# State-space decay rows and attention scores as pairs of 64-row matmuls, a further look-ahead of one pair of heads, and a down projection that waits per gated tile

## What is computed

```python
for i in range(DEPTH_2):                       # 0: griffin_swa, 1: mamba2
    h = h + rms_norm(mixer(rms_norm(h, pre), *mix), post)
    h = h + rms_norm(conv_ffn(rms_norm(h, f_pre), w_up, c_w, c_b, w_down), f_post)

# layer 0, windowed attention: 16 query heads of 64, 2 key heads, window 128, meta tokens, sinks
s_band = jnp.einsum("bnqkgd,bnskd->bnkgqs", qb, k_band) * scale
# layer 1, state space: 32 heads of 64, 8 groups, blocks of 128 tokens
seg = cs_t[..., :, None] - cs_t[..., None, :]
decay_in = jnp.exp(jnp.where(tril, seg, -jnp.inf))
y_diag = jnp.einsum("bcgls,bcghls,bcsghp->bclghp", cb, decay_in, xdt)
# feed-forward
return (jax.nn.gelu(g, approximate=True) * up) @ w_down      # 2816 = 22 tiles of 128
```

## Time and profile before

| | |
|---|---|
| median of three executions | 2697.47 us (2692.95 to 2702.48) |
| the profiled execution | 2703.03 us, span 2701.2 us |
| mean granted clock of TensorE | 0.954 |
| busy: TensorE, VectorE, ScalarE, GpSimd | 2430.9, 762.1, 555.8, 49.5 us |
| windowed attention | about 1724 to 1792 us |
| decay loop | about 2308 to 2372 us |
| starts of the down projections | 2029 and 2611 us |

### The profile page before, as it was taken

How to read it: one execution, slowest core, us unless ns; L and a number is a source line. 1 busy time by engine, 2 the same in 40 slices (tenths; PEclk the granted TensorE clock), 3 DMA queues, 4 the chain that set the end, 5 groups by cost and what they waited for, 6 DMA issues and landing times.

```text
span 2701.2 us, 36383 instructions
## 1 busy us (share of the span) xinstructions
PE 2430.9 (90%) x15128; PEld 1614.7 (60%) x15128; DVE 762.1 (28%) x1853; ACT 555.8 (21%) x1381; POOL 49.5 (2%) x71
## 2 busy tenths in 40 slices
PE   6999997898997978979887778999999999999998
PEld 4685875586442423334323226777887788678887
DVE  1010345532121111111111014733440335624431
ACT  2110112411121211112111113532111221512110
POOL 0000000000000000000000000100000000100000
PEclk9999998997998999999989878989999999989999
DMA  8132252053999998999999994323334333023432
GB/s 319 62 125 94 89 193 107 29 200 142 391 411 421 410 421 371 392 421 420 421 420 421 421 411 178 110 78 124 141 116 145 129 142 139 32 78 126 155 114 90
DMA packets 86935, 608.36 MB, mean 225 GB/s; under 512 B 9552, under 2 KB 11728, under 8 KB 16080
## 3 DMA queue, kind: packets, MB, share of 16 engines
q1 hardware_dynamic: 86224, 602.49, 56.4%
q0 software_dynamic: 400, 2.46, 0.2%
q10 hardware_dynamic: 144, 1.05, 0.1%
HBM read 604.91 MB, written 1.05 MB: 224 GB/s over the span
## 4 chain that ended last, share of the span: by engine, by line
PE 71%; DMA 11%; SPq 10%; DVE 4%; ACT 2%; issue 2%; DVEq 0%; POOL 0%; ACTq 0%
PE bank L532 28%; PE bank L562 10%; SPq L821 10%; PE bank L2309 8%; DMA arena<-in_w_e 7%; PE bank L546 4%; PE bank L2330 3%; DMA ring<-in_w_e 3%; PE bank L2095 2%; PE bank L2259 2%; PE bank L2484 1%; PE bank L2121 1%; DMA ring<-in_w_ada 1%; PE bank L2275 1%; PE bank L2535 1%
## 5 line engine op out<-in xcount | busy, mean ns | idle before, releaser
L532 PE MATMUL bank<-arena,ring 128*128 128x272 f32 (+3 forms) x3200 | 764.0, 401 | 6.1 <-issue 3.0
L532 PEld LDWEIGHTS bank<-arena,ring 128*128 128x128 f32 x3200 | 610.0, 191 | 153.1 <-issue 51.3
L2309 PE MATMUL bank<-arena 128*32 128x512 f32 x2184 | 276.3, 621 | 51.7 <-DMA arena<-in_w_e 51.7
L562 PE MATMUL bank<-arena,ring 128*128 128x272 f32 (+2 forms) x1216 | 280.0, 394 | 6.0 <-DVE arena L1736 6.0
L562 PEld LDWEIGHTS bank<-arena,ring 128*128 128x128 f32 x1216 | 235.9, 194 | 50.3 <-DVE arena L1736 6.9
L1605 DVE TENSOR_TENSOR arena<-bank,arena 128x256 f32<-128x256 f32 x56 | 23.7, 424 | 814.8 <-PE bank L2288 774.3
L2309 PE MATMUL bank<-ring,arena 128*32 128x512 f32 x1400 | 180.2, 626 | 39.3 <-DMA ring<-in_w_e 39.1
L2309 PEld LDWEIGHTS bank<-arena 128*32 128x32 f32 x2184 | 59.9, 111 | 205.9 <-DMA arena<-in_w_e 104.1
L1722 DVE SCALAR_TENSOR_TENSOR arena<-arena,par 128x272 f32<-128x272 f32 (+1 forms) x296 | 148.8, 503 | 10.5
L2330 PE MATMUL bank<-arena 128*32 128x256 f32 x1824 | 116.8, 401 | 27.3 <-DMA arena<-in_w_e 24.1
L1041 ACT ACTIVATE arena<-bank 32x256 f32<-32x256 f32 x224 | 83.9, 374 | 251.0 <-PE bank L2330 248.6
(11 more groups left out here) (403 smaller groups left out, 2174.5 us busy)
## 6 DMA issues: line engine op xcount, KB each, us to landing
arena<-in_w_e SPq DMA_DIRECT2D x222, 1024.0 KB, 25.4
ring<-in_w_e SPq DMA_DIRECT2D x162, 1024.0 KB, 26.0
ring<-in_w_up SPq DMA_DIRECT2D x44, 1024.0 KB, 4.8
ring<-in_w_l SPq DMA_DIRECT2D x37, 1024.0 KB, 4.8
ring<-in_w_ada SPq DMA_DIRECT2D x24, 1024.0 KB, 6.3
ring<-in_w_proj SPq DMA_DIRECT2D x24, 1024.0 KB, 4.8
ring<-in_w_down SPq DMA_DIRECT2D x32, 704.0 KB, 4.0
ring<-in_w_merge SPq DMA_DIRECT2D x16, 1024.0 KB, 4.8
```

Of the source, the lines that this page charges most:

```text
L532: mm = pe.matmul(o[:, a:n], ring[:, s, k * 256 + c * P:k * 256 + (c + 1) * P], rhs(k), start=(k == 0), stop=(k == KT - 1))
L562: mm = pe.matmul(o[:, a:n], ring[:, s, k * P:(k + 1) * P], rhs(part * kt + k), start=(part == 0 and k == 0), stop=(part == parts - 1 and k ...
L2309: mm = pe.matmul(bank[q * GROUP:(q + 1) * GROUP, hidden_bank(g), :], xe[:, (g // CHUNK) % 2, k, s:s + GROUP], w[:, q * 512:(q + 1) * 512], ...
```

## The change

Four edits. (1) The down projections wait for gated tile k ahead of matmul k of the first output, instead of for all tiles at the start. (2) The keys are kept once, `k0`, both key heads on their own 64 partitions; the scores of the two heads of a pair are matmuls over 64 partitions each, issued alternately, and stand ahead of the values of pair j-2. The clears are gone. (3) The decay rows of two heads are matmuls over 64 partitions each, from `csr` and a copy of it on partitions 64 to 95, into four banks; rows 2n+4 and 2n+5 are issued in step n, and both wait for the decays of heads 2n and 2n+1. (4) One matmul and one ScalarE copy more make the copy of `csr`.

```diff
-ROW_BANKS = (2, 3, 6)
+ROW_BANKS = (2, 3, 6, 7)
...
-            for s in range(2):
-                ins = act.activation(kz[64 * s:64 * s + 64, s, :], o[64 * s:64 * s + 64, 0:L], ACT.Copy)
-            ins.then_inc(free, 1)
+            act.activation(k0[:, :], o[:, 0:L], ACT.Copy).then_inc(free, 1)
...
             act.wait_ge(sem("dt_step"), 6)
+            act.activation(csr[64:64 + SH, :], bank[64:64 + SH, 4, 0:L], ACT.Copy)
...
-            pool.memset(kz[64:128, 0, :], 0.0).then_inc(sem("kz_cleared"), 1)
-            pool.memset(kz[0:64, 1, :], 0.0).then_inc(sem("kz_cleared"), 1)
-            pool.wait_ge(sem("kz_cleared"), 2)
...
-                pe.wait_ge(sem("ffn_act"), at.ffn)
                 at.a = a2
-                project_deep(pe, at, 2, FT // 2, lambda k: actF[:, k, a2:], L, done=result_sum, a=a2)
+                project_deep(pe, at, 2, FT // 2, lambda k: actF[:, k, a2:], L, done=result_sum, a=a2,
+                             first=lambda k: pe.wait_ge(sem("ffn_act"), at.ffn - FT + k + 1))
...
+            def swa_scores(j):
+                if j >= 1:
+                    pe.wait_ge(sem("swa_masked"), 2 * j)
+                if j < 8:
                     pe.wait_ge(sem(f"bank_read{(q_read + j) % NL}"), (q_read + j) // NL + 1)
+                for t0 in (0, P) if j < 8 else (0,):
+                    for s in range(2):
+                        half = slice(64 * s, 64 * s + 64)
+                        if j < 8:
+                            mm = pe.matmul(bank[:, (2 * j + s) % 3, t0:t0 + t0 + P], q0[half, j, t0:t0 + P], k0[half, 0:t0 + P],
+                                           start=True, stop=True)
...
                 if j >= 1:
                     swa_turn(2 * j - 2)
+                if j < 9:
+                    swa_scores(j)
                 if j >= 2:
                     swa_values(j - 2)
-                if j < 9:
-                    swa_scores(2 * j)
                 if j >= 1:
                     swa_turn(2 * j - 1)
-                if j < 9:
-                    swa_scores(2 * j + 1)
...
             pe.wait_ge(sem("dt_step"), 4)
+            pe.matmul(bank[64:64 + SH, 4, 0:L], ident[0:SH, 0:SH], csr[0:SH, :], start=True, stop=True)
...
-            def ssm_rows(h):
+            def ssm_ready(h):
...
-                if h >= 3:
-                    pe.wait_ge(sem("ssm_decay"), h - 2)
+                if h >= 4:
+                    pe.wait_ge(sem("ssm_decay"), h - 3)
+
+            def ssm_row_pair(heads):
+                for h in heads:
+                    ssm_ready(h)
                 for c, (t0, n) in enumerate(TOK[0:2]):
+                    for h in heads:
+                        half = slice(64 * (h % 2), 64 * (h % 2) + 64)
+                        mm = pe.matmul(bank[:, ROW_BANKS[h % 4], SEG[c]:SEG[c] + L - t0],
+                                       cst("ident", 64 * (h % 2) + h, 1)[half, :].to_broadcast([64, P]), csr[half, t0:L],
+                                       start=True, stop=True)
+                        if c == 1:
+                            mm.then_inc(sem("ssm_rows"), 1)
...
-            for h in range(3):
-                ssm_rows(h)
+            ssm_row_pair((0, 1))
+            ssm_row_pair((2, 3))
             for n in range(ST):
-                for h in (2 * n + 3, 2 * n + 4):
-                    if h < SH:
-                        ssm_rows(h)
+                if n < ST - 2:
+                    ssm_row_pair((2 * n + 4, 2 * n + 5))
                 pe.wait_ge(sem("ssm_weights"), 2 * n + 2)
```

More of the change, by code:

```diff
@@ L733, in program @@
         q0 = take(KT, T)
-        kz = take(2, L)
+        k0 = take(L)
         q_end = take(8, META)
@@ L1312, in _ @@
                 act.activation(d[:, 144:288], d[:, 144:288], ACT.Exp, bias=csc[:, 0, h:h + 1])
-                act.activation(d[:, 288:416], bank[:, ROW_BANKS[h % 3], 288:416], ACT.Exp, bias=csc[:, 0, h:h + 1])\
+                act.activation(d[:, 288:416], bank[:, ROW_BANKS[h % 4], 288:416], ACT.Exp, bias=csc[:, 0, h:h + 1])\
                    .then_inc(sem("ssm_decay"), 1)
@@ L1897, in ssm_clamp @@
                 dve.tensor_tensor(dec[:, h % DECAYS, 0:288].rearrange("p (a b) -> p a b", a=2),
-                                  bank[:, ROW_BANKS[h % 3], 0:288].rearrange("p (a b) -> p a b", a=2),
+                                  bank[:, ROW_BANKS[h % 4], 0:288].rearrange("p (a b) -> p a b", a=2),
                                   csp[:, :, h:h + 1].to_broadcast([P, 2, 144]), ALU.min).then_inc(sem("ssm_clamped"), 1)
@@ L2539, in _ @@
             q_read = at.out
[L2541 to L2546, removed]
-                    pe.wait_ge(sem(f"bank_read{(q_read + j) % NL}"), (q_read + j) // NL + 1)
[L2548 to L2552, removed]
+            def swa_scores(j):
+                if j >= 1:
+                    pe.wait_ge(sem("swa_masked"), 2 * j)
+                if j < 8:
+                    pe.wait_ge(sem(f"bank_read{(q_read + j) % NL}"), (q_read + j) // NL + 1)
+                for t0 in (0, P) if j < 8 else (0,):
[4 more added lines that the diff above has]
+                                           start=True, stop=True)
+                        else:
+                            mm = pe.matmul(bank[:, (2 * j + s) % 3, 0:L], q_end[half, :, :].rearrange("p j t -> p (j t)"),
+                                           k0[half, :], start=True, stop=True)
+                        if t0 == P or j == 8:
+                            mm.then_inc(sem("swa_scores"), 1)
             def swa_turn(i):
@@ L2577, in swa_values @@
                 mm.then_inc(sem("swa_pv"), 1)
-            pe.wait_ge(sem("kz_cleared"), 2)
             for j in range(10):
@@ L2650, in ssm_rows @@
                     pe.wait_ge(sem("cb_read"), 1)
-                if h >= 3:
-                    pe.wait_ge(sem("ssm_decay"), h - 2)
-                for c, (t0, n) in enumerate(TOK[0:2]):
-                    mm = pe.matmul(bank[:, ROW_BANKS[h % 3], SEG[c]:SEG[c] + L - t0],
-                                   cst("ident", h, 1).to_broadcast([P, P]), csr[:, t0:L],
-                                   start=True, stop=True)
-                mm.then_inc(sem("ssm_rows"), 1)
+                if h >= 4:
[3 more added lines that the diff above has]
+                    ssm_ready(h)
+                for c, (t0, n) in enumerate(TOK[0:2]):
+                    for h in heads:
[5 more added lines that the diff above has]
+                            mm.then_inc(sem("ssm_rows"), 1)
             def group_sum(n):
```

## The result

The changed kernel takes 2672.11 us (median of four executions, 2669.44 to 2673.34); the kernel before, timed on the same chip, took 2697.81 (2692.95 to 2702.48). The ratio is 0.9904, with a 95% interval of 0.9884 to 0.9923. In microseconds, one minus the ratio times 2697.8, that is 25.9 us less, with an interval of 20.8 to 31.3. The forecast was 21.1 us less, 2676.4.

What follows compares the result with a forecast made beforehand. TensorE, busy 90% of the span, was taken as the bound, with a circle of waits in the decay loop. Savings 7.7 + 9.8 - 0.6 + 4.2 = 21.1 us off 2697.5 gave 2676.4 us, range 2667 to 2690.

Steps and rivals of the forecast that it cites:

- The circle of 3.61 us: Decay loop before: values and group sum, row, clamp, weights, values wait on each other in turn, 3.61 us.
- Part 1: Down projections: per-tile waits remove 6.0 us of standstill and 1.7 us of half clock, 7.7 us saved.
- Part 2: Pairs of 64 rows: two heads cost what one does, 0.8 us in the loop; each tile-shape change costs 0.1.
- the rival price of about 0.4 us: Tile-mode change drains one whole matmul, 0.4 us; each loop step loses about 0.6 more, half the gain goes.
- Part 3: Decay loop: pairs and rows issued a step earlier cut 52.0 us to 42.6; with the start, 9.8 us saved.
- the handing over: Decay loop: an allowance of 0.1 us a step for passing work between engines, making the step 3.0 us.
- VectorE's 2.6 a step: Decay loop: VectorE's 38.86 us of work in 15 steps, the next limit; as pace in every step, bound 13 saved.
- Part 4: Copy of csr for the upper rows: one more 272-column matmul where TensorE has no rest, 0.6 us lost.
- Part 5: Windowed attention: paired scores ahead of values, keys copied once; steps 6.35 instead of 6.64 us, 4.2 us saved in all.
- (a): Decay loop held by reading out and handing over, not TensorE; step 3.25 us, time 2680; chance 0.19.
- (b): The 64-row pairs don't overlap; only 2 us gained in the loop, time 2689; chance 0.06.
- (c): Granted clock falls to the lower level within the decay loop, adding 37.5 us; time 2714; chance 0.04.

Runs made afterwards that it cites:

- e5: The kernel before with the decay loop's four banks and further look-ahead, but each row still over all 128 partitions: 2691.60 us, ratio 0.9972.
- e1: The kernel before with only the down projections' wait changed to one per gated tile: 2689.04 us, ratio 0.9970.
- e3: The kernel before with only the attention part: keys kept once, paired scores ahead of the values: 2694.31 us, ratio 0.9992.
- e2: The kernel before with only the decay-loop part: 64-row pairs, four banks, one pair further ahead, copy of csr: 2680.67 us, ratio 0.9949.
- e4: The changed kernel run again without edits, on the same chip as its three separate parts: 2672.43 us, ratio 0.9905 to the kernel before.
- e10: The changed kernel run again without edits, beside the values-ahead-of-scores version: 2672.52 us, ratio 0.9912 to the kernel before.
- e8: The kernel before with only the attention order changed, both full-row scores ahead of the values: 2699.33 us, ratio 1.0009.
- e7: The changed kernel with values ahead of the paired scores again, except the last scores: 2668.93 us, ratio 0.9887 to the kernel before.
- e9: The kernel of e7 run again without edits, beside the changed kernel: 2667.18 us, ratio 0.9882 to the kernel before.
- values first: The changed kernel with attention values ahead of the paired scores except the last, run as e7 and e9: 2668.93 and 2667.18 us.
- e6: The kernel of e2 with row pairs 2n+2 and 2n+3 issued in step n, so pairing without look-ahead: 2740.12 us, ratio 1.0153 to the kernel before.

## Why the prediction was right

The range, 2667 to 2690, held the time, and the forecast was 4.3 us above it. Point by point:

**What bounds the kernel.** Right: TensorE set the pace in the loop and in attention, and each part's gain appears in the time. The circle of 3.61 us was right in size (step of 3.60 before), but it held only every second step; e5 shows that TensorE's own work, 3.89, held the others.

**Part 1, 7.7 us: measured 8.0** by the trace (3.3 + 4.7), 8.1 by e1's ratio. The whole wait went, the 44 added waits cost nothing that can be seen, and the half clock behind the second projection went with the standstill. The first projection gave 0.3 more than the 3.0 of its wait. That it shows no fall of the clock held for the kernel before; e3's fell there as well, for 3.4 us.

**Part 2, the pair at 0.8 and a change of 0.1: measured 0.91** from the pair's start to the values. Two heads cost what one does, with 0.97 us for eight records. As for the drain that the Trainium skill names (TensorEngine Tiling (Array Packing), section Tiling Modes), the run decides: it is inside that 0.91. The same columns of one head take 0.70, which leaves 0.2 at most for the change, so the rival price of about 0.4 us isn't borne out.

**Part 3, 9.8 us: measured 11.2.** The first term to be off is the four steps without a group sum: I let VectorE hold them at 2.8, 11.2 us; they took 1.98 + 3.06 + 2.28 + 3.06 = 10.38. The second is the handing over, 0.1 a step. With a pair's lead there is none, and nine steps took 26.0 us instead of 27.0. The last two, 2.67 and 1.93, were 0.25 longer than I said. Together 0.8 + 1.0 - 0.25 = 1.6 us more, and the start gave 0.2 instead of 0.4: there TensorE has a new wait of 1.0 us for VectorE's mask (line 1904) ahead of the next group's scores, the wait that I had taken to cost nothing. VectorE's 2.6 a step did not become the bound: its 37.13 us fit into 41.00. It still waited for rows, 6.3 us in all, but TensorE waited for its weights only three times.

**Part 4, 0.6 lost: measured 0.** The timeline of TensorE in the changed kernel, where the copy for the upper rows (line 2610) stands beside the 512-column matmul (line 2611):

```profile
2168.66 0.41 PE L2610 MATMUL bank<-arena,con 32*32 32x272 f32 x1
2168.67 0.60 PE L2611 MATMUL bank<-small,con 32*16 32x512 f32 x1
2168.92 0.39 PE L2610 MATMUL bank<-arena,con 32*32 32x272 f32 x1
2169.11 0.59 PE L2611 MATMUL bank<-small,con 32*16 32x512 f32 x1
...
2170.05 0.50 PE L532 MATMUL bank<-arena,ring 128*128 128x272 f32 x1
```

The first records of the two start 0.01 us apart, and the copy's second has ended (2169.31) before the other's second does (2169.70). They write to different output partitions (64 to 95, and 0 to 15), and the stretch from the first of them to the next projection is 1.39 us, as before (1.38 from the 2181.01 of the earlier trace rows). I had priced the copy as standing in line. The Trainium skill, TensorEngine Tiling (Array Packing), section Tiling Modes, says that tiles operate independently; the rows agree for two tiles that share their input rows.

**Part 5, 4.2 us: measured about 3.0.** The stage from the key copy to the first out-projection matmul takes 72.1 us before (72.5 in e1, 71.8 in e2) and 69.8, 69.9, 68.7 and 68.1 in the four kernels that have the change (the changed kernel, e4, e10, e3), 3.0 less in the mean; e3's ratio says 2.2. The term that was mis-sized is the step: 0.12 instead of 0.29. I had the scores start 0.05 us behind the end of the query copy; they start 0.14 behind it (1741.44 against 1741.12 + 0.18). And I forgot the change of shape between values and second transposes, which take 0.38, not 0.33. 5 x 0.17 = 0.85 of the 1.2 us missing. The tail, from the transposes right behind the last query tile to the out projection, is 1.6 us shorter in the mean (15.1 to 16.9 us in these four, 17.4 to 18.1 in the three before), where my terms for it make 1.85, and varies with the half clock in it. It came out about as worked: TensorE waited 2.61 us instead of 2.90, the paired last scores follow the transposes, and the second mask comes 1.14 behind the first, where it was 1.55. The changed kernel's tail in the timeline (2550 the last scores, 1803 the masks):

```profile
1772.31 0.90 PE L2562 MATMUL bank<-con,arena 128*128 128x128 f32 x3 [2.61 <-DVE arena L1821]
...
1773.14 1.28 PE L2550 MATMUL bank<-arena 64*128 64x272 f32 x4
...
1774.45 0.50 DVE L1803 SCALAR_TENSOR_TENSOR arena<-con,bank 128x272 f32<-128x272 f32 x1 [0.90 <-PE bank L2550]
...
1775.59 0.49 DVE L1803 SCALAR_TENSOR_TENSOR arena<-con,bank 128x272 f32<-128x272 f32 x1
```

**The sum.** 8.0 + 11.2 + 0 + 3.0 = 22.2 us stand in the traces, beside 25.9 by the ratio; the ratio's interval, 20.8 to 31.3, holds both. One thing that lies in between is visible. Behind the loop TensorE stands still for the reciprocal of the group norm, 2.96 us, before and after alike, and then the granted clock is 0.50. How long differs. Busy time by stretch there, first of the kernel before:

```profile
2375.00:2392.10 17.10, 16.38 (x36) 11.65 (x37) 7.58 (x17) 0.00 (x0) 0.00 (x0) 0.52 0.00 1
```

then of the changed kernel:

```profile
2352.40:2366.00 13.60, 13.60 (x31) 9.34 (x31) 6.91 (x16) 0.00 (x0) 0.00 (x0) 0.50 0.00 0
```

and of e1, which has the loop of before:

```profile
2368.60:2375.40 6.80, 6.80 (x17) 4.90 (x16) 4.66 (x12) 0.00 (x0) 0.00 (x0) 0.50 0.00 0
```

It was 17.1 us in the profiled executions of before, e3 and e8, 13.7 in the changed kernel and e7, 10.2 in e5, and 6.8 in e1, e2, e4, e9 and e10. The changed kernel and e4 are the same code and have 13.7 and 6.8, so it is not a property of the code alone. Half of it is lost time: (17.1 - 13.7) / 2 = 1.7 us of the profiled difference, up to 5.1 for the others. It may be that the change makes the short ones likelier; one profiled execution for each kernel can't show that. The mean granted clock, which is on record for all but a few of the executions, bears on it: 0.9543 over 41 of the kernel before, 0.9563 over 13 of the changed one, 0.9581 over 8 of values first. One minus the clock, times the span, is the time withheld: 123, 117 and 112 us, give or take 1 to 2. The stretch behind the second down projection makes 1.7 us of the first difference of 6. So the changed kernel seems to run at a slightly higher clock elsewhere too. By an estimate from all these executions, among those of one kernel 1 us more withheld goes with some 0.3 us more time; the other 4 to 5 us would then make some 1.4 of the 3.7 us between the traces and the ratio. In which stretches they lie, and what makes up the rest, stays open.

**The rivals.** (a) did not happen: no value matmul waits for weights except three times, once early and at the last two pairs, 1.6 us in all. (b) did not happen; e5, which comes close to it, gains 4.1 us in the loop where I had said 2 for (b). (c) did not happen to this kernel. It did to e6, where TensorE works at half clock through most of the loop; the loop of 80 us that my price meant (42.6 + 37.5) became 99.8 there, since at the lower clock the circle grows too, which (c) had left out.

## What to carry to other kernels

When matmuls use only half of the input rows, two of them on different halves and into different banks cost what one costs (0.97 us for either here); but take the lead first, because a pair is one lump of work, and a loop that pairs without issuing a step further ahead may stand still longer than it saves. Put a matmul whose operand another engine has just begun to copy behind work that is ready, not ahead of it: values before scores made each attention step 0.38 us shorter than the reverse. Where an accumulation takes its tiles in the order in which they are made, a wait for all of them can become a wait for each tile in the first output, and what it saves is the wait and the half clock behind it (3.0 + 1.7 us at the second projection).

## What the runs showed of the hardware

- A loop in which TensorE stood still 2 to 3 us in each step of 5 to 8 us ran at a mean granted clock of 0.59 and took 99.8 us for work that takes 41.0 with 1.6 us of standstill in all.
- The half-clock stretch behind one and the same standstill of 2.96 us was 6.8 us long in two profiled executions (e4, e10) and 13.7 in another of the same code.
- A 272-column float32 matmul from 32 rows to 32 columns of the array ran beside a 512-column one from the same 32 rows to 16 other columns, and the stretch that holds both was 0.01 us longer than without it (1.39 against 1.38).
